# Six changes of order in a two-block transformer kernel: unit roundings, squares, K, masks and attention staging

## The reference, cut to what matters

```
h = h + 0.5 * swiglu(rmsnorm(h), wg, wu, wd)             # FFN1, inner width 2816
u = rmsnorm(h) @ w_in                                    # queries, keys, values, gates
o = [nsa_attention(8 heads, three branches), forgetting_attention(8 heads)]
h = h + rmsnorm(o) @ w_out
h = h + 0.5 * swiglu(rmsnorm(h), ...)                    # FFN2
h = h + sigmoid(rmsnorm(h) @ ple_w_gate) * rmsnorm(p @ ple_w_proj)   # "PLE gate"
# second block: 16 meta tokens in front, 528 tokens
proj = rmsnorm(h) @ w_in_2                               # q, f, i, gates, convolution inputs
f = lb + (1 - lb) * sigmoid(f_raw); k = 1 - f            # HGRN2 recurrence with decay f
h = h + merged(hgrn2(q, k, v, log f), conv) @ w_out_2
h = h + (silu(conv(a) + b) * val) @ w_down_2             # FFN3, with a convolution
out = rmsnorm(h)[:, 16:]
```

## Time and profile before

| what | value |
|---|---|
| runs of the kernel | 2238.88, 2241.16, 2243.03 us, median 2241.16 |
| profiled execution | 2241.53 us, its span 2239.6 us, mean granted TensorE clock 0.988 |
| TensorE busy | 2169.7 us, 97% of the span |
| DVE, ScalarE, GpSimd busy | 865.0, 751.0, 895.7 us (39, 34, 40%) |

### The profile page before, as it was taken

The page is one execution under the profiler, slowest core; times in us unless marked ns, Lnnn a source line. Parts: engine busy times, 40 slices in busy tenths (PEclk is TensorE's granted clock), DMA queues, the critical chain, the costliest instruction groups (busy, mean ns, idle before and its releaser), DMA issues.

```text
span 2239.6 us, 32464 instructions
## 1 busy us (share of the span) xinstructions
PE 2169.7 (97%) x12772; PEld 1894.5 (85%) x12772; DVE 865.0 (39%) x1281; ACT 751.0 (34%) x1102; POOL 895.7 (40%) x691
## 2 busy tenths in 40 slices
PE   8999999999998999999999999999998999999998
PEld 6788888777887778888888999999997798989887
DVE  4222201676665522223027322232229454565402
ACT  4333212425667423333124332212210433333213
POOL 3444444335221444444444344444330133444442
PEclk9999999999999999999999999999999999999999
DMA  5223222521000222332222222222210012222321
GB/s 159 94 94 94 94 94 94 159 78 57 20 2 1 85 75 94 94 94 94 95 93 76 88 84 92 94 94 76 94 57 1 20 39 93 93 95 83 105 94 56
DMA packets 152171, 178.95 MB, mean 80 GB/s; under 512 B 6949, under 2 KB 142478, under 8 KB 152094
## 3 DMA queue, kind: packets, MB, share of 16 engines
q1 hardware_dynamic: 151931, 177.83, 24.4%
q10 hardware_dynamic: 163, 0.04, 0.0%
HBM read 175.76 MB, written 2.10 MB: 79 GB/s over the span
## 4 chain that ended last, share of the span: by engine, by line
PE 63%; issue 21%; POOL 11%; DVE 3%; DMA 0%; ACT 0%; SPq 0%; POOLq 0%; DVEq 0%; ACTq 0%
PE ps L1779 40%; PE ps L1919 11%; POOL wlo L650 11%; PE ps L2284 3%; PE ps L2190 2%; PE ps L2312 2%; PE ps L2160 1%; PE ps L2173 1%; PE ps L2031 1%; DVE tmp L1185 1%; DMA raw<-in_ffn_wu 0%; DVE Ad L1664 0%; PE ps L2241 0%; PE ps L2318 0%; PE ps L2010 0%
## 5 line engine op out<-in xcount | busy, mean ns | idle before, releaser
L650 POOL TENSOR_TENSOR wlo<-raw,whi 128x512 fp32r<-128x512 f32 x634 | 832.0, 1345 | 1190.1 <-ACT whi L737 1096.7
L1779 PE MATMUL ps<-xh,whi 128*128 128x512 f32 (+2 forms) x2432 | 703.5, 335 | 10.7 <-POOL wlo L650 9.1
L1779 PE MATMUL ps<-xh,wlo 128*128 128x512 f32 (+2 forms) x2432 | 701.0, 334 | 0.0
L1779 PE MATMUL ps<-xl,whi 128*128 128x512 f32 (+2 forms) x2432 | 698.0, 333 | 0.0
L737 ACT ACTIVATE whi<-raw 128x2048 fp32r<-128x2048 f32 (+1 forms) x158 | 301.2, 1906 | 773.1 <-PE ps L1779 467.2
L1779 PEld LDWEIGHTS ps<-xh,whi 128*128 128x128 f32 x2432 | 415.5, 189 | 63.1 <-POOL wlo L650 10.1
L1779 PEld LDWEIGHTS ps<-xh,wlo 128*128 128x128 f32 x2432 | 414.2, 189 | 47.1 <-issue 1.9
L1779 PEld LDWEIGHTS ps<-xl,whi 128*128 128x128 f32 x2432 | 414.2, 189 | 45.8
L1919 PE MATMUL ps<-act_h,whi 128*128 (+1 forms) x528 | 209.2, 396 | 0.0
L1919 PE MATMUL ps<-act_l,whi 128*128 (+1 forms) x528 | 208.9, 396 | 0.0
L1919 PE MATMUL ps<-act_h,wlo 128*128 (+1 forms) x528 | 208.2, 394 | 0.0
(11 more groups left out here) (318 smaller groups left out, 2480.1 us busy)
## 6 DMA issues: line engine op xcount, KB each, us to landing
raw<-in_w_in SPq DMA_DIRECT2D x47, 1024.0 KB, 5.1
raw<-in_ffn_wg SPq DMA_DIRECT2D x22, 1024.0 KB, 5.3
raw<-in_ffn_wu SPq DMA_DIRECT2D x22, 1024.0 KB, 5.4
raw<-in_ffn_wd SPq DMA_DIRECT2D x22, 1024.0 KB, 4.9
raw<-in_w_up SPq DMA_DIRECT2D x22, 1024.0 KB, 5.1
raw<-in_w_down SPq DMA_DIRECT2D x11, 1024.0 KB, 4.8
raw<-in_w_out SPq DMA_DIRECT2D x8, 1024.0 KB, 4.9
raw<-in_ple_w_gate SPq DMA_DIRECT2D x4, 1024.0 KB, 4.9
```

Of the source, the lines that this page charges most:

```text
L650: last = nc.gpsimd.tensor_tensor(wlo[:, slot, d], raw[:, slot, d], whi[:, slot, d].bitcast(F32), ALU.subtract)
L1779: last = mm(ps[:, j * banks + b, 0:n], w[:, k, e * P:(e + 1) * P], x[:, k, c0:c0 + n], start=(k == 0 and q == 0), stop=(k == KD - 1 and q ...
```

## The change

It reorders instructions; no arithmetic changes. (1) At the start GpSimd converts the masks behind `lo(2)` and `lo(3)`, and TensorE's sums and spread of the first norm stand at slices 6 and 4 and not 2 and 2. (2) In the three up projections the rounding of the fourth unit stands ahead of step 0, right behind the root. (3) In the PLE gate a small Sqrt loads the table early, six of the eight squares stand ahead of `root(3)`, and `rsqrt(3)` behind five additions. (4) `K` is made in four parts ahead of the rounding of unit W_IN2+37, `Ad` is cleared in two halves with a semaphore count each, and TensorE waits for the last part of V only at head 3. (5) In the attention the two roundings of q stand one block earlier, both roundings of k behind an `otok` product of the second block, and GpSimd's subtraction for q waits for `o_done`. The semaphore `am_zero` counts the clearing of `Am`.

```diff
@@ gpsimd
             lo(1, 1)
+            lo(2, 0)
+            lo(3, 1)
             pool.wait_ge(ident_in, 16)
             pool.wait_ge(masks_in, 48)
             for dst, src in ((levelmask, levels_f), (causal, causal_f), (cmpneg, cmpneg_f), (ident_b, ident)):
                 nc.gpsimd.tensor_copy(dst[:], src[:]).then_inc(setup, 1)
-            lo_run(2, W_IN1 + 1)
+            lo_run(4, W_IN1 + 1)
...
             for n in range(2, NH):
+                pool.wait_ge(o_done, PER_HEAD * (n - 1) + 2)
                 q_lo_of(n, qs, U_QA, q_hi, q_lo)
...
-            nc.gpsimd.memset(Ad[:], 0.0).then_inc(az, 1)
+            for g in range(2):
+                nc.gpsimd.memset(Ad[:, HG * g:HG * (g + 1), :], 0.0).then_inc(az, 1)
@@ scalar, ffn_up
-                    hi_at(first, 3, i)
+                    if not (ahead and isinstance(i, int) and i == 0):
+                        hi_at(first, 3, i)
...
-                with act.Fori(0, F // UC - 1) as i:
+                step(0, True)
+                hi_one(first + 4)
+                if g == 0:
+                    act.wait_ge(setup, 7)
+                with act.Fori(1, F // UC - 1) as i:
                     step(i, True)
                     hi_at(first, 4, i)
...
             root(0, 1)
+            hi_one(3)
...
-            act.wait_ge(setup, 7)
             ffn_up(0, W_UP1, ahead=1)
...
                     if 1 <= n < NH - 1:
+                        if (i, b) == (BLOCKS[1], 0):
+                            stage_q(n + 1)
                         if (i, b) == (BLOCKS[1], 1):
-                            stage_q(n + 1)
-                        if (i, b) == (BLOCKS[2], 0):
                             stage_fox_q(n + 1)
...
             root(2, 1)
+            hi_one(W_UP2 + 3)
             act.wait_ge(pT_done, 2)
...
             hi_one(W_PLG + 1)
-            root(3, 1, 8)
+            nc.scalar.activation(warm[:, 2:3], epsc[:], ACT.Sqrt).then_inc(warmed, 1)
             for n in range(KD):
+                if n == 6:
+                    root(3, 1, 8)
                 square_of(4, n, h[:, n, M:T], M, 2)
...
-            for u in range(W_IN2 + 35, W_IN2 + 38):
+            for u in range(W_IN2 + 35, W_IN2 + 37):
                 hi_one(u)
...
-            for g in range(2):
-                heads = slice(HG * g, HG * (g + 1))
+            for g in range(VH // 2):
+                heads = slice(2 * g, 2 * g + 2)
                 nc.scalar.activation(K[:, heads, :], Fg[:, heads, :], ACT.Copy, scale=-1.0, bias=1.0).then_inc(k_made, 1)
+            hi_one(W_IN2 + 37)
...
             root(6, 0)
+            hi_one(W_UP3 + 3)
@@ vector
-                        if (i, b) == (BLOCKS[2], 1):
-                            stage_fox_k(n + 1, (0,))
-                        if (i, b) == (BLOCKS[2], FOX):
-                            stage_fox_k(n + 1, (1,))
-                        if (i, b) == (BLOCKS[3], 0) and n + 3 < NH:
+                        if (i, b) == (BLOCKS[0], FOX) and n + 3 < NH:
                             stage_fox_c(n + 3)
...
+                    if 1 <= s // PER_HEAD < NH - 1 and (i, b) == (BLOCKS[1], 0):
+                        stage_fox_k(s // PER_HEAD + 1)
...
-            rsqrt(3, 1, 8)
             for n in range(1, KD):
+                if n == 6:
+                    rsqrt(3, 1, 8)
                 add_square(4, n, M, 2)
...
-            nc.vector.memset(Am[:], 0.0).then_inc(az, 1)
-            dve.wait_ge(az, 2)
+            nc.vector.memset(Am[:], 0.0).then_inc(am_zero, 1)
+            dve.wait_ge(am_zero, 1)
...
+                    if lv < 0:
+                        dve.wait_ge(az, 1 + g)
                     select(lv, HG * (g + 1) - 1)
@@ tensor
-                        if k == 2 and e == 0:
+                        if k == at_[0] and e == 0:
                             sums()
-                        if k == 2 and e == 1 and kept is None:
+                        if k == at_[1] and e == 1 and kept is None:
                             spread_()
...
-            second_unit(0, 0, lambda: norm_sums(0, True), lambda: norm_spread(0, True))
+            second_unit(0, 0, lambda: norm_sums(0, True), lambda: norm_spread(0, True), at_=(6, 4))
...
-            pe.wait_ge(vev, 4)
+            pe.wait_ge(vev, 3)
...
-                    pe.wait_ge(k_made, 2 if n == META else n // HG + 1)
+                    pe.wait_ge(k_made, VH // 2 if n == META else n // 2 + 1)
+                    if n == 3:
+                        pe.wait_ge(vev, 4)
```

More of the change, by code:

```diff
@@ L447, in build @@
         k_made = sem("k_made")
+        am_zero = sem("am_zero")
         amx_mm = sem("amx_mm")
@@ L1819, in opening, with second_unit @@
                 second_unit(u, p, sums, spread_, banks, splits, kept, xs)
-            def second_unit(u, p, sums, spread_, banks=1, splits=(WHOLE, WHOLE), kept=None, xs=X):
+            def second_unit(u, p, sums, spread_, banks=1, splits=(WHOLE, WHOLE), kept=None, xs=X, at_=(2, 2)):
                 pe.wait_ge(lo_ready, u + 2)
```

## The result

The changed kernel takes 2204.94 us at the median of four runs (2203.14 to 2207.17), the kernel before 2240.02 us on the same chip; the ratio is 0.9842, 95% interval 0.9825 to 0.9859. Forecast were 2209.5 us, range 2201 to 2222. The profiled execution has a span of 2201.4 us against 2239.6: 38.2 us less, where the medians lie 35.1 apart. The profiled execution of the changed kernel is the fastest of its four, that of the kernel before (2241.53 us) lies above its median, so some 3 us of the 38.2 lie in which two executions were profiled. The mean granted clock of the two is 0.998 and 0.988.

The account below looks back on a forecast made before the run. TensorE's waits and clock were taken to bound the kernel. Terms summing to 31.4 us, off the profiled 2241.5, gave 2210.1; with the median 0.4 lower, 2209.7, and 2209.5 was predicted, range 2201 to 2222.

Parts of the forecast that it names:

- What bounds: Whole kernel: TensorE works nearly throughout, so the end moves only with its waits and its clock.
- Start, 5.5: First norm: later sums remove a 2.42 us wait for the adds and 3.1 us lost at low clock.
- Fourth unit in FFN1 and FFN2, 4.2 and 6.1: Up projections: earlier rounding removes `wlo` waits of 2.73 and 3.37 us and the low clock behind them.
- FFN3, 1.1: Third up projection: earlier rounding removes a 1.12 us wait; gain between 0 and 1.1, taken as 1.1.
- Rival (E): FFN3: delayed silus and a table load make every later rounding late, kernel slower, 2250 at 4 us a pass; chance 0.03.
- Gate, 5.6: PLE gate: squares ahead of the root save 2.5 us of a 3.10 us wait and 3.1 us at low clock.
- K, 5.8: First level: K in quarters ahead of the rounding brings DVE's first multiply forward; 5.8 us at full clock, 3.8 at low.
- Attention, 3.1: Six heads: staging moves remove 6.4 us of `otok` waits, of which 3.3 come back as `probT` waits.
- About 0.55 us a head come back as waits for `probT`: Attention: q stagings in ScalarE's fullest stretch cost 3.3 us over six heads.
- rival (B): Whole kernel: waits go but the low clock stays, 12.4 us less gain, 2222, or 2216 with half; chance 0.22.

Follow-up runs that it names:

- the last version: Changed kernel plus later sums of the mix norm and of the norm ahead of W_IN2, K in eight parts, and q's roundings one block later: 2198.50 us.
- the second: Changed kernel plus sums of the mix norm and of the norm ahead of W_IN2 at slice 4, K in eight parts; repeat run: 2200.03 us.

## Why the prediction was right, step by step

- What bounds: TensorE's waits and clock. Right: with the same 12772 products TensorE's busy time fell by 19.3 us, from 2169.7 to 2150.4, and its idle time by the other 18.9 of the 38.2 us. The first is the low clock: ten stretches, 47.8 us in all, ahead of the kernel's last microseconds before, two of 6.8 us in all after, and 45% of the difference is 18.5 us.
- Start, 5.5: measured 5.8. That the later place of the sums is enough is shown: with it, masks early or late differ by 0.1 us. But undoing the sums alone cost only 1.4 us, since the wait then is 1.08 us and not 2.42 (masks late: the seven adds take 6.39 and not 7.16 us; and TensorE arrives 1.0 us later, the adds start only 0.4 later) and has no low clock behind it. So the masks' place does give something where the sums stand early; how much of the remaining 4 us is its doing, and how much the low clock's coming and going, no run separates.
- Fourth unit in FFN1 and FFN2, 4.2 and 6.1: measured 4.6 and 6.4. FFN3, 1.1: 1.4. Rival (E) fell: TensorE has no wait in the later passes of the loops, and the shift stays at 38.2 through FFN3.
- Gate, 5.6: 5.8. The wait left is 0.34 us, under the 0.5 to 0.8 that I gave: I had taken 8.4 us for all seven adds beside GpSimd, and the last two ran behind its subtractions (1.49 us for two, 5.92 for the five ahead).
- K, 5.8: 4.4. The term was mis-sized, though TensorE started where I said: I counted 16 products for four heads at 0.144 us. The rows show 64 for the eight heads of a level, 8 a head, 32 for four, at 7.38/64 = 0.115; from 1632.93 that ends at 1636.6, and the multiply follows at 1637.41, 4.5 us after TensorE's start and not 3.0.
- Attention, 3.1: 6.0, over the six heads alone 6.3. This is the step that failed: "About 0.55 us a head come back as waits for `probT`". The waits for `probT` didn't change. Nearly all 6.4 us of the `otok` waits went; the new place of ScalarE's stagings costs 1.4 us at small `otok` waits. So the result lies under the forecast partly because this loss was priced at 3.3.
- The low clock: rival (B) fell. I had priced the five stretches beside moved instructions and none of the other five in the trace of before. Four of these went or shrank: three gave 1.3, 1.5 and 1.5 us, the one at 1692 nothing. The waits at them are as long as before, so these 4.3 us come not from the waits that the change removes but from where the low clock falls, and for the forecast they are luck. In the other kernels short waits have it again: with the attention as before at 401 and 1217, with q's roundings late at 1209.
- The sum came out 6.8 us short of the span's 38.2: 4.3 are those stretches, 2.9 the attention, -1.4 K, and 1.0 small ones at the start, the fourth units and the gate. Against the median, 2204.94, the forecast of 2209.5 is 4.6 us too high.

## What to carry to other kernels

Price a removed wait with the low clock behind it, where the trace shows one, but don't count on it to the microsecond: waits of 1 to 3 us had it in some profiles and not in others, even with the same instructions around them. To find what an order of instructions is worth, compare the start of the same product in both traces, place by place; it separates terms of 1 us that the time of the whole can't. Where a tiny operation of DVE is long, look at what GpSimd does beside it, and move its feeder (here a rounding of k) rather than the operation.

## What the runs showed of the hardware that was not expected

Between the start and the last microseconds of each profile the low clock comes in stretches of 3.41 or 6.83 us. The two pairs of profiles of one kernel have them behind the same waits, even behind waits of 0.6 to 1.3 us. Yet the length of a wait doesn't decide it. Waits of 2.5 us (fourth unit late, FFN1) and 3.12 us (K behind the rounding) have no stretch; the wait of 3.95 us at the end of the attention has one in all 14 profiles. The wait of 1.3 us at the mix norm is in eleven of them: in four a stretch follows, and there the products ahead of it start 1.35, 1.66, 1.99 and 4.05 us later than in the changed kernel; in the five that are 0 to 0.84 us later, and in the two of the kernel before (10.0 and 10.7 us later), none follows. What in this time decides is open, as no run moved a wait in time and nothing else.
Both kernels with q's roundings late ran W_IN2 faster, at a full clock and with no wait in either. Windows of the last version (above) and of the second, without that move (below):

```profile
1300.00:1500.00 200.00, 200.00 (x1646) 200.00 (x1646) 56.27 (x76) 42.24 (x34) 88.55 (x68) 1.00 0.29 94
```

```profile
1300.00:1500.00 200.00, 200.00 (x1636) 200.00 (x1636) 55.82 (x75) 42.21 (x34) 88.49 (x68) 1.00 0.29 92
```

1646 products of the same shape against 1636 in 200 us are 0.6% more; over 350 us of W_IN2 it comes to 1.8 us. Both profiles with the move have it, none of the other twelve (1636 or 1637). The cause is open: the edit touches another engine's instructions several hundred microseconds earlier.
